# A fused Fourier and retention layer: second channel halves of five token tiles, and a sixth tile, loaded channel-major and scaled by rows of factors

## The reference

```python
mod_x = jax.nn.silu(c) @ w_ada[l] + b_ada[l]
mod_c = jax.nn.silu(c_ctx) @ w_ada[l] + b_ada[l]
h_x = _modulate(_rms_norm(x, norm1_gain[l]), sh1, sc1)
h_c = _modulate(_rms_norm(ctx, norm1_gain[l]), csh1, csc1)
u, q, k, v, g, ga, gb = jnp.split(h_x @ w_in, list(IN_SPLITS), axis=-1)
...
def _rms_norm(x, gain):
    y = xf * lax.rsqrt(jnp.mean(xf * xf, axis=-1, keepdims=True) + EPS)
def _modulate(h, shift, scale):
    return h * (1.0 + scale) + shift
```

## Time and profile before

| | |
|---|---|
| median of 3 runs | 1266.64 us (1266.29 to 1267.78) |
| profiled execution, its own time | 1267.94 us |
| its span in the trace | 1266.1 us |
| TensorE busy | 1244.4 us, 98% |
| VectorE busy | 884.2 us, 70% |
| ScalarE busy | 608.1 us, 48% |
| GpSimd busy | 163.9 us, 13% |
| HBM read, written | 168.76 MB, 51.39 MB |

### The profile page before, as it was taken

How to read it: one execution, slowest core, us unless ns; L and a number is a source line. 1 busy time by engine, 2 the same in 40 slices (tenths; PEclk the granted TensorE clock), 3 DMA queues, 4 the chain that set the end, 5 groups by cost and what they waited for, 6 DMA issues and landing times.

```text
span 1266.1 us, 16896 instructions
## 1 busy us (share of the span) xinstructions
PE 1244.4 (98%) x6192; PEld 1028.7 (81%) x6192; DVE 884.2 (70%) x1388; ACT 608.1 (48%) x1043; POOL 163.9 (13%) x112
## 2 busy tenths in 40 slices
PE   6999999999999999999999999999999999999997
PEld 3778888888998888888888888888888888888886
DVE  4572487758669988787687766566545669769866
ACT  6761211235436443443678555455455443544544
POOL 0115420142250000125410000000000000000000
PEclk9999999999999999999999999999999999999999
DMA  9614230103286456587633544444448985577634
GB/s 370 247 34 148 85 100 1 34 20 100 69 292 223 146 188 204 203 340 249 255 128 117 180 160 142 153 163 142 150 167 281 314 288 180 167 234 261 189 104 160
DMA packets 95802, 221.27 MB, mean 175 GB/s; under 512 B 11596, under 2 KB 11996, under 8 KB 95720
## 3 DMA queue, kind: packets, MB, share of 16 engines
q1 hardware_dynamic: 83328, 184.80, 43.6%
q10 hardware_dynamic: 8728, 22.29, 4.9%
q0 software_dynamic: 3664, 13.11, 3.2%
HBM read 168.76 MB, written 51.39 MB: 174 GB/s over the span
## 4 chain that ended last, share of the span: by engine, by line
PE 62%; DVE 2%; issue 1%; ACT 1%; DMA 0%; ACTq 0%; DVEq 0%
PE ps L3054 8%; PE ps L3055 8%; PE ps L3056 8%; PE ps L3691 8%; PE ps L3699 8%; PE ps L3694 8%; PE ps L3717 3%; PE ps L3531 3%; PE ps L3526 3%; PE ps L3528 3%; PE ps L3137 0%; PE ps L3592 0%; PE ps L3599 0%; PE ps L3593 0%; DMA ada_next<-in_ada_columns 0%
## 5 line engine op out<-in xcount | busy, mean ns | idle before, releaser
L3054 PE MATMUL ps<-t_hi,s_hi 128*128 128x512 f32 x392 | 153.2, 391 | 0.0
L3055 PE MATMUL ps<-t_lo,s_hi 128*128 128x512 f32 x392 | 153.0, 390 | 0.0
L3056 PE MATMUL ps<-t_hi,s_lo 128*128 128x512 f32 x392 | 153.0, 390 | 0.0
L1834 ACT ACTIVATE s_hi<-s_raw 128x512 fp32r<-128x512 f32 x112 | 70.5, 630 | 114.4 <-DMA b<-in_w_stream 59.0
L1076 POOL TENSOR_TENSOR ring_lo<-raw,ring_hi 128x1024 fp32r<-128x1024 f32 (+2 forms) x37 | 87.3, 2370 | 202.2 <-ACT ring_hi L1202 198.7
L2933 DVE TENSOR_TENSOR s_lo<-s_raw,s_hi 128x512 fp32r<-128x512 f32 x112 | 77.2, 690 | 44.0 <-ACT s_hi L1834 43.6
L3054 PE MATMUL ps<-ring_hi,hT_hi 128*128 128x512 f32 x224 | 90.8, 405 | 1.3 <-issue 1.3
L3056 PE MATMUL ps<-ring_hi,hT_lo 128*128 128x512 f32 x224 | 87.6, 391 | 0.0
L3055 PE MATMUL ps<-ring_lo,hT_hi 128*128 128x512 f32 x224 | 87.4, 390 | 0.0
L3054 PEld LDWEIGHTS ps<-t_hi,s_hi 128*128 128x128 f32 x392 | 73.6, 188 | 16.0 <-DVE t_lo L2937 0.2
L3056 PEld LDWEIGHTS ps<-t_hi,s_lo 128*128 128x128 f32 x392 | 73.6, 188 | 15.9
(11 more groups left out here) (513 smaller groups left out, 3194.0 us busy)
## 6 DMA issues: line engine op xcount, KB each, us to landing
s_raw<-ff_scr SPq DMA_DIRECT2D x112, 256.0 KB, 3.0
raw<-in_w_stream SPq DMA_DIRECT2D x34, 512.0 KB, 4.1
ff_scr<-ffs SPq DMA_DIRECT2D x16, 1024.0 KB, 4.8
t_raw<-in_w_stream SPq DMA_DIRECT2D x64, 256.0 KB, 3.4
w_B_raw<-in_w_stream SPq DMA_DIRECT2D x48, 256.0 KB, 2.7
ff_scr<-ffa SPq DMA_DIRECT2D x16, 768.0 KB, 4.5
b<-in_w_stream SPq DMA_DIRECT2D x48, 256.0 KB, 4.4
ada_next<-in_ada_columns POOLq DMA_DIRECT2D x13, 512.0 KB, 4.3
```

The costliest lines, as they stand in the source:

```text
L1834: A(s_slot[n][0][:], s_slot[n][2][:], ACT.Copy).then_inc(down_hi, 1)
L3054: M(dst, lhsT=l_hi, rhs=r_hi, start=first, stop=False, skip_group_check=goes_on)
L3055: M(dst, lhsT=l_hi, rhs=r_lo, start=False, stop=False, skip_group_check=goes_on)
L3056: return M(dst, lhsT=l_lo, rhs=r_hi, start=False, stop=last, skip_group_check=goes_on)
```

## The change

- The second halves of tiles 0 to 4 are loaded with channels on partitions as well, from a new host copy `x_halves`, five loads of 256 KB into a part of the buffer that later holds tiles 6 to 9. They wait for the first modulation product (`ada_done` 1) and stand on SP ahead of the fourth chunk of key weights.
- Tile 5 is loaded like tiles 6 to 9: rows for the squares, columns into a buffer of its own (`x_fifth`).
- TensorE makes rows of factors for tiles 0 to 3 at once (`rstd_rows(0, 3)`, where tile 0's second-half transposes stood) and for tiles 4 and 5 (`rstd_rows(4, 5)`, after the first pass of tile 2's second half). The transposes of second halves and of tile 5 are gone.
- VectorE scales each half by its row (`scale_half`, new); the first of these stands before `mod_columns(1)` and waits for all five loads. The second halves of tiles 1 to 4 are modulated on ScalarE and tile 0's on VectorE as before, now from SBUF. Tile 5 goes through `scale_columns` and `modulate_columns`.
- `norm` covers 512 channels instead of 1024, and tile 5's is gone.
- On ScalarE the rounding of the first two value-weight chunks is split: one after `square(7)`, one after `square(9)`, instead of both together before tile 8's modulation.
- The first tile of the values, of the queries and of the gates runs its hi times lo pass last (`first_tile`, new).
- `load_rows` of tiles 6 to 8 waits for first-half transposes, as there are no others.

```diff
-SIDE = [("x", _s, 0) for _s in range(EARLY)] + [("x", _s, 1) for _s in range(EARLY)]
-SIDE += [("x", EARLY, _h) for _h in range(2)] + [("xs", _s) for _s in range(EARLY + 1, 10)]
+SIDE = [("x", _s, 0) for _s in range(EARLY)] + [("rw", 0), ("rw", 1)]
+SIDE += [("xs", _s) for _s in range(EARLY + 1, 10)]
...
+        def load_half(eng, s):
+            if s == 0:
+                eng.wait_ge(ada_done, 1)
+            eng.dma_start(half_tile(s), ins["x_halves"][s]).then_inc(halves_in, 16)
...
+                if i == 3:
+                    for s in range(EARLY):
+                        load_half(sp, s)
                 if i in (2, 3):
                     sp.dma_start(raw_of(i), ins["w_stream"][WIDX[(kind, n)]]).then_inc(k_in[i - 2], 16)
                     continue
                 if i == 4:
-                    load_x(sp, 5)
+                    load_rows(sp, 5)
+                    load_columns(sp, 5)
...
             def norm(s):
                 act.wait_ge(rstd_ready, s + 1)
-                A(x_tile(s), x_tile(s), ACT.Identity, scale=rstd[:, s:s + 1]).then_inc(xhat, 1)
+                A(x_tile(s)[:, 0:512], x_tile(s)[:, 0:512], ACT.Identity, scale=rstd[:, s:s + 1]).then_inc(xhat, 1)
...
             def modulate(n):
...
                 for q in range(4):
                     c = 4 + q
-                    ins_ = A(dst[:, q, :], ps[:, side_bank(key), q * P:(q + 1) * P], ACT.Identity,
+                    ins_ = A(half_buf(n)[:, q, :], half_tile(n)[:, q * P:(q + 1) * P], ACT.Identity,
                              scale=a1[:, c, r:r + 1], bias=mod[:, c, r:r + 1])
...
             for s in range(6, 15):
-                if s == 6:
-                    modulate(5)
-                elif s <= 10:
+                if s <= 10:
                     modulate_columns(s - 1)
                 if s <= 10:
                     h_his(s - 1)
                 if s < 9:
                     square(s + 1)
+                    if s in (6, 8):
+                        hi_to(("v", (s - 6) // 2))
                     root_of(s + 1)
                 if s > 6:
                     copy_kt(s - 7)
-                if s == 8:
-                    hi_to(("v", 1))
...
+            def scale_half(s):
+
+                dve.wait_ge(side_done, SIDX[row_key(s)] + 1)
+                dve.wait_ge(halves_in, 16 * EARLY)
+                x3 = half_tile(s).rearrange("p (c t) -> p c t", c=4)
+                ins_ = V.tensor_tensor(x3, x3, row_of(s).to_broadcast([P, 4, P]), ALU.mult)
+                if s == 3:
+                    ins_.then_inc(side_free[SIDX[("rw", 0)] % 2], 1)
                 else:
+                    ins_.then_inc(half_scaled, 1)
...
+            def first_tile(kind, dst, l_hi, l_lo, middle):
+
+                for kp in range(4):
+                    c = (kind, kp)
+                    pe.wait_ge(hi_done, INDEX[c] + 1)
+                    r_hi, _ = slot(c)
+                    for e in range(2):
+                        kt = 2 * kp + e
+                        cols_ = slice(e * 512, (e + 1) * 512)
+                        M(dst, lhsT=l_hi[:, kt, :], rhs=r_hi[:, cols_], start=kt == 0, stop=False)
+                        M(dst, lhsT=l_lo[:, kt, :], rhs=r_hi[:, cols_], start=False, stop=False)
+                if middle is not None:
+                    middle()
+                for kp in range(4):
+                    _, r_lo = chunk((kind, kp))
...
+            def rstd_rows(first, last):
+
+                key = row_key(first)
+                pe.wait_ge(rstd_ready, last + 1)
+                side_wait(pe, key)
+                for s in range(first, last + 1):
+                    mm = M(row_of(s)[:, 0, :], lhsT=rstd[:, s:s + 1].to_broadcast([P, P]), rhs=ident[:], start=True, stop=True)
+                mm.then_inc(side_done, 1)
...
-            x_transposes(0, (1,))
+            rstd_rows(0, 3)
             for kt in range(KT):
                 ada_part(1, kt)
             k_part(3, 0, ("hh",))
             row_transposes(1)
             k_part(3, 0, ("lh", "hl"))
-            x_transposes(1, (1,))
-            k_part(4, 0, ("hh", "lh"))
-            x_transposes(2, (1,))
-            k_part(4, 0, ("hl",))
+            k_part(4, 0, ("hh", "lh", "hl"))
             for n in range(EARLY):
-                k_part(n, 1, ("hh", "lh", "hl"), lambda: x_transposes(n + 3, (1,) if n < 2 else (0, 1)) if n < 3
-                       else rstd_row(6) if n == 4 else None)
+                k_part(n, 1, ("hh", "lh", "hl"), lambda: rstd_rows(4, 5) if n == 2 else rstd_rows(6, 6) if n == 4 else None)
```

More of the change, by code:

```diff
@@ L177, in program @@
         x_last = place("x_last", o_kv + 12288, [P, D])
+        x_fifth = place("x_fifth", o_kv + 4096, [P, D])
+        half_cols = place("half_cols", o_ht, [P, KT, D])
         ctx_in = place("ctx_in", o_kv, [P, 2, D])
@@ L746, in x_tile, with half_tile, row_key, row_of @@
         def x_tile(s):
-            return ctx_in[:, s, :] if s < 2 else x_a[:, s - 2, :] if s < 6 else x_b[:, s - 6, :]
+            return ctx_in[:, s, :] if s < 2 else x_a[:, s - 2, :] if s < 5 else x_b[:, s - 6, :] if s > 5 else x_fifth[:]
+        def half_tile(s):
+            return half_cols[:, s, 512:1024]
+        def row_key(s):
+            return ("rw", s // 4) if s < 6 else ("xs", s)
+        def row_of(s):
+            return ps[:, side_bank(row_key(s)), None, (s % 4 if s < 6 else 0) * P:((s % 4 if s < 6 else 0) + 1) * P]
+        def half_scaled_wait(eng, s):
+            if s == 3:
+                side_out(eng, ("rw", 0))
+            else:
+                eng.wait_ge(half_scaled, s + 1 if s < 3 else 4)
         def ada_b_part(kt):
@@ L1273, in h_his @@
                 hv = h_f[:].rearrange("p (c t) -> p c t", c=KT)
-                if n == EARLY:
-                    for half in range(2):
-                        side_out(act, ("x", n, half))
-                else:
-                    act.wait_ge(first_mod, n - EARLY)
-                    act.wait_ge(second_mod, n - EARLY)
+                act.wait_ge(first_mod, n - EARLY + 2)
+                act.wait_ge(second_mod, n)
                 A(hi_ap, hv, ACT.Copy).then_inc(hhi_done, 1)
@@ L2030, in _, with modulate @@
                 tokens_rstd(s)
-            def modulate(n, half):
-                key = ("x", n, half)
+            def modulate(n):
+                key = ("x", n, 0)
                 r = 1 if n < 2 else 0
                 dve.wait_ge(side_done, SIDX[key] + 1)
-                if n < EARLY:
-                    if half:
-                        dve.wait_ge(h_ready, EARLY - n % 2)
-                        if n > 1:
-                            dve.wait_ge(h_ready, EARLY + n - 1)
-                    elif n > 1:
-                        dve.wait_ge(h_ready, n - 1)
-                    dst = half_buf(n)
-                else:
-                    dve.wait_ge(h_ready, EARLY + n)
-                    dst = h_f[:, 0:512].rearrange("p (c t) -> p c t", c=4)
-                for q in range(4):
-                    c = 4 * half + q
-                    ins_ = V.tensor_scalar(dst[:, q, :], ps[:, side_bank(key), q * P:(q + 1) * P], a1[:, c, r:r + 1],
-                                           mod[:, c, r:r + 1], ALU.mult, ALU.add)
-                ins_.then_inc(side_free[SIDX[key] % 2], 1)
+                if n > 1:
+                    dve.wait_ge(h_ready, n - 1)
+                for q in range(4):
+                    ins_ = V.tensor_scalar(half_buf(n)[:, q, :], ps[:, side_bank(key), q * P:(q + 1) * P], a1[:, q, r:r + 1],
+                                           mod[:, q, r:r + 1], ALU.mult, ALU.add)
+                ins_.then_inc(side_free[SIDX[key] % 2], 1)
@@ new lines, in modulate_half @@
+            def modulate_half(n):
+                r = 1 if n < 2 else 0
+                half_scaled_wait(dve, n)
+                dve.wait_ge(h_ready, EARLY - n % 2)
+                for q in range(4):
+                    c = 4 + q
+                    ins_ = V.tensor_scalar(half_buf(n)[:, q, :], half_tile(n)[:, q * P:(q + 1) * P], a1[:, c, r:r + 1],
+                                           mod[:, c, r:r + 1], ALU.mult, ALU.add)
+                ins_.then_inc(first_mod, 1)
+            def scale_half(s):
[3 more added lines that the diff above has]
+                ins_ = V.tensor_tensor(x3, x3, row_of(s).to_broadcast([P, 4, P]), ALU.mult)
+                if s == 3:
+                    ins_.then_inc(side_free[SIDX[("rw", 0)] % 2], 1)
+                else:
+                    ins_.then_inc(half_scaled, 1)
@@ L2144, in _ @@
             tokens_rstd(3)
-            modulate(2, 0)
+            modulate(2)
             first_lo(2)
@@ L2148, in _ @@
             tokens_rstd(4)
-            modulate(3, 0)
+            modulate(3)
             first_lo(3)
-            modulate(4, 0)
+            modulate(4)
             first_lo(4)
+            scale_half(0)
             mod_columns(1)
-            modulate(0, 1)
+            modulate_half(0)
+            scale_half(1)
```

(16 more changed lines are left out.)

89 lines of the change are left out of this document (42 added, 47 removed).

## The result

| | before | changed |
|---|---|---|
| median, six runs each | 1267.31 us (1266.29 to 1269.93) | 1275.10 us (1272.11 to 1279.12) |
| ratio, 95% interval | | 1.0065 [1.0053, 1.0076] |
| profiled execution, its span | 1267.94, 1266.1 us | 1279.12, 1277.3 us |

The change makes the kernel about 8 us **slower**; forecast were 1266.0 us and at most 1268.0. The profiled execution is the slowest of the six, so the trace shows somewhat more loss than the median has.

The account below looks back on a forecast made before the run. TensorE, busy 98% of the span, was taken to bound the kernel: 2.18 us of work and a 1.3 us wait go, 2.9 us of new waits come, leaving 0.6 us gained. Forecast median 1266.0 us, range 1262.9 to 1268.0.

Parts of the forecast that it names:

- The step that failed first: VectorE, key stage: modulating tile 0's second half from SBUF was left at its old price, the same four operations.
- The second step: ScalarE, tiles 6 to 9: split roundings fit its waits, so the 1.3 us TensorE wait before tile 8 goes.
- The rival of the clock: TensorE: new waits of 2.9 us drop its clock to half rate, losing 2.9 us, 1268.9 us; chance 0.06.
- the prediction's signs of being wrong: Tile 5 near 60.4; copy after 42; four-product groups at 1.9 us after 60; new wait at first value, query or gate tile.
- ScalarE and the tiles: Key stage: ScalarE's 7.8 us chain for tiles 4 and 5 sets the pace; tile 5 starts at 61.55, tile 6 at 69.54.
- 2.9 us of new waits: TensorE, key stage: waits of about 1.2 us before tile 5, on ScalarE, and again before tile 6, on VectorE.
- The gain of 0.6 us from tile 8: TensorE starts tile 8's keys at 81.8 instead of 82.4, and these 0.6 us carry to the end.
- Loads: Half-tiles land at 39.8 us, making the modulation-row copy 0.4 us late and costing TensorE 0.1; other delayed loads stay hidden.
- The later stages: Behind the key stage: later waits as before, and reordered first tiles of values, queries and gates give nothing.
- TensorE's added rows: Key stage: six row products cost 1.04 us, four in tile 0's old place 0.66 us of it.
- The full gain: Rival: ScalarE and VectorE keep ahead, so 2.18 + 1.3 = 3.5 us come out, 1263.1 us; chance 0.14.

Follow-up runs that it names:

- experiment 3: Changed kernel with GpSimd's remainder of the last key weights made to wait for the modulation of tile 0's second half: 1275.17 us, ratio 1.0060.
- experiment 2: Changed kernel with ScalarE's roundings of the first two value weights put back together, as in the kernel before: 1272.41 us, ratio 1.0043.
- experiment 1: Changed kernel with products that compute nothing put into TensorE's two long waits, before tiles 6 and 7: 1272.33 us, ratio 1.0045.
- experiment 4: Changed kernel with the two value-weight roundings together again and GpSimd's remainder of the last key weights after tile 0's second-half modulation: 1270.47 us, ratio 1.0029.
- experiment 10: Changed kernel with VectorE's copy of the modulation rows put ahead of the first scaling: 1274.85 us, ratio 1.0048.

## Why the prediction was wrong

**The step that failed first**: "The modulation of tile 0's second half is the same four operations with an SBUF source; I leave it at its price." It took 3.30 us, and tiles 5 to 7 start some 1.4 us later for it (experiment 3). The source was the difference: from PSUM the four ran beside GpSimd at full price, from SBUF they were stopped (experiment 3 takes GpSimd away: 1.12 us). The clue stood in the earlier trace rows, and the prediction used it as a price: a remainder of 1.48 us, where the same operation takes 1.22.

The Trainium skill (SBUF — State Buffer, "SBUF: two separate sides") says that VectorE and GpSimd share a pair of ports, "an exclusive lock, not a bandwidth split": a VectorE operation contends for it in a 2-port mode, or with two SBUF inputs if GpSimd's operation reads SBUF, and whichever starts first holds it for the whole instruction. The runs here agree: modulations from SBUF and remainders from two SBUF operands stretched to GpSimd's end, scalings with one operand in PSUM never did. In which mode the modulations ran no run shows.

**The second step**: "one now stands in its 1.60 us wait, the other in the like wait two tiles on, so tile 8 is no longer held by them." ScalarE's time was free, but GpSimd makes the remainder right behind each rounding, and this was not followed. The remainders fell on the modulation of tile 6 and, once the clock had fallen, on the remainder of tile 7; undone, 2.7 us come back, the clock's share among them (experiment 2).

**The rival of the clock** was given 0.06 and 2.9 us. It happened as a consequence, twice in the profiled execution, for 3.0 us; filling the waits gives 2.8 us back (experiment 1). Of the prediction's signs of being wrong it is the one that came, in another form: four products take 1.7 us behind 72.60, 0.43 us each. The argument against it, one wait of 1.29 us without a fall, held only for waits of that size.

**ScalarE and the tiles** were right as a mechanism and in size: in experiment 4 tiles 5 to 7 start within 0.1 us of the forecast. Counted were 2.9 us of new waits; the changed kernel has 7.6 us of waits in the key stage, GpSimd and the clock behind the difference. The gain of 0.6 us from tile 8 could not come, since it rested on the split.

**Loads**: the last half landed at about 40.2 us, not 39.8, and TensorE lost 1.05 us before the row transposes where 0.1 was counted. In the other versions of the same order the first scaling starts between 39.80 and 40.85 us, and TensorE loses from nothing to 2.0 us. Later waits take most of that back, as long as there are any (experiment 10).

**The later stages**: "later waits as before" missed that an odd change in the number of side results exchanges their banks (0.5 us of wait at 668.89). TensorE's added rows were priced too low: the first four hold it for 1.06 us, not 0.66.

**The full gain** was out of reach for this order; another order gets most of it. With GpSimd's remainders off VectorE's path, the row of tile 4 early and two moves in the cycle, the kernel is 0.17% [0.08, 0.26] faster than before, about 2.2 of the 3.5 us.

What stays open: why version 3 gains nothing in the median, the price of the exchanged banks, and why the clock falls behind some of these waits and not behind others.

## What to carry to other kernels

When an operand moves from PSUM to SBUF, or a weight rounding moves in time, look at what GpSimd does in that stretch and in the one it moves to: VectorE's row gets longer there, and no view of waits says so. A wait that grows past what the trace has shown can cost more than its length, because TensorE's clock may fall behind it. And where a list gives out banks in turn, count its entries before and after.
